# The state-space layer's output projection in three reduced-precision passes, with each group's y turned in the next group

## The reference

```python
zxbcdt = u @ w_in
z, xbc, dt = jnp.split(zxbcdt, [SSD_D_INNER, SSD_D_INNER + SSD_CONV_DIM], axis=-1)
xbc = jax.nn.silu(causal_depthwise_conv(xbc, conv_w, conv_b))
xs, bm, cm = jnp.split(xbc, ...)          # 4 groups: x 512 wide, B and C 128 wide each
...
y = y_diag + y_off + d_skip[:, :, None] * xs
y = y.reshape(bsz, seq, SSD_D_INNER) * jax.nn.silu(z)
y = rms_norm(y.reshape(bsz, seq, g_, SSD_D_INNER // g_), norm_w)   # per group of 512
return y @ w_out                                                   # (512x2048) @ (2048x1024)
...
h = layer_norm(DEEPNORM_ALPHA * x + mix, ln_g[i, 0], ln_b[i, 0])
h = layer_norm(DEEPNORM_ALPHA * h + sq_relu_mlp(h, mlp_w1[i], mlp_w2[i]), ...)
```

## Time and profile before

| | |
|---|---|
| time, median of 3 runs | 2157.13 us (2156.45 to 2160.23) |
| the profiled execution | 2160.06 us, span of its instructions 2158.3 us |
| PE busy with matmuls | 2008.8 us (93%) |
| DVE, ACT, POOL busy | 1040.1, 839.7, 171.7 us |
| mean granted clock of PE | 0.96 |

### The profile page before, as it was taken

The page is one execution under the profiler, slowest core; times in us unless marked ns, Lnnn a source line. Parts: engine busy times, 40 slices in busy tenths (PEclk is TensorE's granted clock), DMA queues, the critical chain, the costliest instruction groups (busy, mean ns, idle before and its releaser), DMA issues.

```text
span 2158.3 us, 26047 instructions
## 1 busy us (share of the span) xinstructions
PE 2008.8 (93%) x9466; PEld 1559.4 (72%) x9466; DVE 1040.1 (48%) x1863; ACT 839.7 (39%) x1703; POOL 171.7 (8%) x137
## 2 busy tenths in 40 slices
PE   8899998999999999988989698999999969989998
PEld 6778786448888887788888677888887745447773
DVE  4665565034444345366677655443436352035643
ACT  5654563023333333365757624232333320114430
POOL 0100110021000003000100021000002000001100
PEclk9999999999999999999999898999999979998999
DMA  4121122222323221241311022232322212110010
GB/s 163 59 98 39 59 98 98 77 72 105 110 85 107 87 104 53 59 118 40 79 39 66 33 78 98 79 117 78 117 78 78 88 51 98 37 65 1 0 39 39
DMA packets 116541, 161.30 MB, mean 75 GB/s; under 512 B 6021, under 2 KB 57059, under 8 KB 116451
## 3 DMA queue, kind: packets, MB, share of 16 engines
q1 hardware_dynamic: 115155, 155.38, 21.6%
q0 software_dynamic: 1296, 4.72, 0.6%
HBM read 157.98 MB, written 2.10 MB: 74 GB/s over the span
## 4 chain that ended last, share of the span: by engine, by line
PE 83%; DVE 8%; ACT 5%; issue 2%; DVEq 1%; DMA 1%; ACTq 0%; SPq 0%; POOLq 0%; POOL 0%
PE psum L900 38%; PE psum L664 9%; PE psum L854 7%; PE psum L985 7%; PE psum L1140 4%; PE psum L629 4%; PE psum L1221 2%; PE psum L1175 2%; PE psum L1017 2%; PE psum L1188 2%; PE psum L964 1%; PE psum L799 1%; ACT fT L1278 1%; DVE w_lo L1938 1%; PE psum L1152 1%
## 5 line engine op out<-in xcount | busy, mean ns | idle before, releaser
L1938 DVE TENSOR_TENSOR w_lo<-slot,w_hi 128x512 fp32r<-128x512 f32 x304 | 213.1, 716 | 382.8 <-ACT w_hi L1421 382.8
L1421 ACT CAST w_hi<-slot 128x512 fp32r<-128x512 f32 x304 | 183.6, 619 | 449.0 <-PE psum L900 448.3
L900 PE MATMUL psum<-f_hi,w_hi 128*128 128x512 f32 (+1 forms) x576 | 215.3, 374 | 19.2 <-DVE f_lo L1945 12.6
L900 PE MATMUL psum<-f_lo,w_hi 128*128 128x512 f32 (+1 forms) x576 | 214.4, 372 | 0.0
L900 PE MATMUL psum<-f_hi,w_lo 128*128 128x512 f32 (+1 forms) x576 | 214.4, 372 | 0.0
L900 PE MATMUL psum<-w_hi,hid_hi 128*128 128x512 f32 x512 | 199.5, 390 | 0.0
L900 PE MATMUL psum<-w_hi,hid_lo 128*128 128x512 f32 x512 | 199.2, 389 | 0.0
L900 PE MATMUL psum<-w_lo,hid_hi 128*128 128x512 f32 x512 | 199.2, 389 | 0.0
L900 PEld LDWEIGHTS psum<-f_hi,w_hi 128*128 128x128 f32 x576 | 112.9, 196 | 38.0 <-DVE f_lo L1945 13.5
L629 PE MATMUL psum<-con,arena 128*128 128x128 f32 (+2 forms) x678 | 105.0, 291 | 33.7 <-ACT arena L1345 13.0
L900 PEld LDWEIGHTS psum<-f_lo,w_hi 128*128 128x128 f32 x576 | 113.0, 196 | 17.3
(11 more groups left out here) (295 smaller groups left out, 4031.7 us busy)
## 6 DMA issues: line engine op xcount, KB each, us to landing
slot<-in_w_mlp SPq DMA_DIRECT2D x128, 512.0 KB, 5.5
slot<-in_w_ssd SPq DMA_DIRECT2D x32, 512.0 KB, 6.3
slot<-in_w_hgrn SPq DMA_DIRECT2D x32, 512.0 KB, 6.6
slot<-in_w_ssd_out SPq DMA_DIRECT2D x16, 512.0 KB, 5.3
slot<-in_w_gate SPq DMA_DIRECT2D x16, 512.0 KB, 5.6
gb<-in_w_ssd SPq DMA_DIRECT2D x8, 512.0 KB, 5.3
slot<-in_w_hgrn_out SPq DMA_DIRECT2D x8, 512.0 KB, 5.2
slot<-in_w_mla SPq DMA_DIRECT2D x8, 512.0 KB, 5.2
```

Source lines behind the costliest of these rows:

```text
L900: m = pe.matmul(psum[:, bank[c], cols or slice(0, HALF)], a, m_, start=k == 0 and n_pass == 0, stop=k == KD - 1 and n_pass == 2)
L1421: act.copy(w_hi[:, k, :], as_k(slot_of(stage, n))[:, k, :]).then_inc(high_made, 1)
L1938: dve.tensor_tensor(w_lo[:, k, :], as_k(slot_of(stage, n))[:, k, :], w_hi[:, k, :].bitcast(F32), ALU.subtract).then_inc(low_made, 1)
```

## The change

Four things change together.

- **The projection** (`ssd_out` in place of `out_and_norm`) is made in three passes. The gain `norm_w` goes into the weights: ACT rounds w times the gain of its row (`out_high`), DVE makes the remainder (`out_low`). Unit 0 takes y of groups 0 and 1 for the first half of the output, by token tile; unit 1 groups 2 and 3, block by block; units 2 and 3 the same for the second half.
- **y** stays in `xr`. Each group's root, reciprocal and normalising are done at the group's end, and PE turns the group's y in the next group behind its first x block (`y_turn`); ACT and DVE copy two chunks each into `yT_a` and `yT_b` (`y_out`). The fourth group's y is turned between units 0 and 1. ACT and DVE split `yT` into high and low parts. `Mh` moves to the memory of `rn`, where y was kept.
- **B and C** are fetched when the group before has begun its first x block, a unit earlier. The sums 0 to 3 stand a block later, and "CB" and "BT" behind the third x block; on DVE the z remainders and the taps of the third x block come ahead of the mask of "CB" and the first four `weights`.
- **Behind the projection** the first MLP unit is split ahead of the last token tile, as at the later layers, and `p` is fetched and turned within the first MLP unit.

The core of the diff:

```diff
@@ banks
+            banks.stage(f"ssd{g}", [("B", 0), ("C", 1), (("x", 0), 2), (("acs", 0), 4), (("acs", 1), 5)]
+                        + [(("yt", c), (6, 7, 0, 1)[c]) for c in range(NT) if g] + [(("x", 1), 3), (("acs", 2), 6), (("acs", 3), 7),
...
+        banks.stage("ssd_out", [((0, t), b) for t, b in enumerate((1, 5, 6, 7))] + [(("yt", c), (4, 2, 3, 4)[c]) for c in range(NT)]
+                    + [((1, t), b) for t, b in enumerate((0, 2, 3, 1))])
-        in_parts = ("mlp0", "gate0", "hgrn_out", "mlp1", "gate1")
+        in_parts = ("ssd_out", "mlp0", "gate0", "hgrn_out", "mlp1", "gate1")
@@ SP
             for g in range(1, S_GROUPS):
+                sp.wait_ge(units_begun, 2 * g - 1)
+                load_bc(g)
                 sp.wait_ge(units_begun, 2 * g)
-                load_bc(g)
                 load_half(g, 0, S_X)
@@ PE
+            def y_turn(stage, g):
+                for c in range(NT):
+                    pe.wait_ge(sig("y_normed"), g * NT + c + 1)
+                    b = claim(stage, ("yt", c))
+                    for k in range(4):
+                        m = turn(b, k * P, xr[:, c, k * P:(k + 1) * P])
+                    m.then_inc(bank_full[b], 1)
...
+                feature_block(("x", 0), "x01", x01, 0, True)
                 spread_sums(0)
                 spread_sums(1)
-                feature_block(("x", 0), "x01", x01, 0, True)
+                if g:
+                    y_turn(stage, g - 1)
+                feature_block(("x", 1), "x01", x01, P, False)
                 spread_sums(2)
                 spread_sums(3)
-                feature_block(("x", 1), "x01", x01, P, False)
+                feature_block(("x", 2), "x23", x23, 0, True)
...
-                feature_block(("x", 2), "x23", x23, 0, True)
                 x_turn(0)
+                feature_block(("x", 3), "x23", x23, P, False)
                 spread_sums(4)
-                feature_block(("x", 3), "x23", x23, P, False)
                 x_turn(1)
...
+            def ssd_out(n, **results):
+                h, part_ = n // 2, n % 2
+                times_parts("ssd_out", n, lambda t, k: (yT_hi[part_][:, k, t * P:(t + 1) * P], yT_lo[part_][:, k, t * P:(t + 1) * P],
+                                                        w_hi[:, k, :], w_lo[:, k, :]),
+                            lambda t: ("ssd_out", (h, t)), opens=part_ == 0, closes=part_ == 1,
+                            ready=None if h else lambda k: pe.wait_ge(sig("yT_low"), part_ * KD + k + 1), **results)
+            for t in range(NT):
+                ssd_out(0, cs=(t,), begins=t == 0, ends=t == NT - 1)
+            y_turn("ssd_out", S_GROUPS - 1)
+            ssd_out(1)
+            ssd_out(2)
+            last_turn = norm_turns("norm00", lambda t: ssd_out(3, cs=(t,), begins=t == 0, ends=t == NT - 1))
@@ ACT
+            def out_high(n, k):
+                if k == 0:
+                    landed(act, "ssd_out", n)
+                if n:
+                    act.wait_ge(blocks_begun, (n - 1) * KD + (k + 2))
+                row = B_SN + (n % 2) * KD + k
+                act.mul(w_hi[:, k, :], as_k(slot_of("ssd_out", n))[:, k, :], col_b[:, row:row + 1]).then_inc(high_made, 1)
@@ DVE, at a group's end
-                    dve.tensor_tensor(ys[c][:, g * HALF:(g + 1) * HALF], ybuf, zs[:, c, :], ALU.mult).then_inc(sig("y_gated"), 1)
+                    dve.tensor_tensor(xr[:, c, :], ybuf, zs[:, c, :], ALU.mult).then_inc(sig("y_gated"), 1)
+                dve.wait_ge(sig("ssq_ready"), NT * (g + 1))
+                dve.tensor_scalar(srs[:, 0, g, :], ssq[:, g, :], 1.0 / HALF, RMS_EPS, ALU.mult, ALU.add).then_inc(sig("sms_ready"), 1)
                 if g + 1 < S_GROUPS:
                     ssd_low(g + 1, "x01")
+                dve.wait_ge(sig("srs_ready"), g + 1)
+                dve.reciprocal(srs[:, 0, g, :], srs[:, 1, g, :])
+                dve.drain()
+                for c in range(NT):
+                    dve.tensor_scalar(xr[:, c, :], xr[:, c, :], srs[:, 0, g, c:c + 1], None, ALU.mult).then_inc(sig("y_normed"), 1)
+                if g + 1 < S_GROUPS:
                     ssd_low(g + 1, "x23")
```

More of the change, by code:

```diff
@@ L474, in slot_free @@
                     sp.sem_inc(sig("slot_given"), 1)
-                elif stage == "mlp0" and n == 1:
-                    wait_full(sp, "ssd_out", NT - 1, NHALF - 1)
                 elif stage == "hgrn_out" or stage == "hgrn" and per:
@@ L537, in _ @@
                     if h == n == 0:
-                        for i in range(DEPTH):
-                            sp.dma_start(s_p[i], p[i].rearrange("(t p) n -> p t n", p=P)).then_inc(p_in, 16)
                         sp.wait_ge(sig("inputs_used"), 1)
@@ L551, in load_mlp @@
                 up(0, 0, 0)
+                if i == 0:
+                    for j in range(DEPTH):
+                        sp.dma_start(s_p[j], p[j].rearrange("(t p) n -> p t n", p=P)).then_inc(p_in, 16)
                 up(0, 1, 0)
@@ L787, in ssd_group @@
                 z_tile(3)
+                if g == S_GROUPS - 1:
+                    wait_taken(pe, stage, ("z", NT - 1))
+                    pe.sem_inc(sig("inputs_used"), 1)
                 wait_taken(pe, stage, "BT")
@@ L863, in times_out @@
                         tile(t)
-            def out_and_norm(stage, norm, left, n_units_):
-                tile = times_out(stage, left, n_units_, 0)
-                for t in range(NT):
-                    tile(t)
-                return norm_turns(norm, times_out(stage, left, n_units_, 1))
-            last_turn = out_and_norm("ssd_out", "norm00", lambda k, t: yT[t][:, k, :], 2)
             inputs_split = [0]
@@ L1493, in ple @@
                         act.activation(sg[:, t, h * HALF:(h + 1) * HALF], psum[:, b, :], ACT.Sigmoid).then_inc(bank_free[b], 1)
-            norm("norm00", B_G, B_B, parts=True, meanwhile=lambda: split_high("mlp0", follows=False))
+            norm("norm00", B_G, B_B, parts=True, before_last=lambda: split_high("mlp0"))
+            for i in range(DEPTH):
+                for k in range(KP):
+                    b = full("p_turn", ("p", i, k))
+                    act.copy(pT[:, i, k, :], psum[:, b, :]).then_inc(bank_free[b], 1)
             mlp(0)
@@ L1822, in ssd_group @@
                 taps(2, ("x", 0), 4 * g)
+                if g:
+                    for c in (1, 3):
+                        y_out(stage, g - 1, c)
                 taps(3, ("x", 1), 4 * g + 1)
+                ssd_low(g, "z")
+                taps(4, ("x", 2), 4 * g + 2)
                 b = full(stage, "CB")
@@ L1854, in ssd_group @@
                     dve.drain()
+                if g == S_GROUPS - 1:
+                    for k in range(KD):
+                        out_low(0, k)
+                        yT_parts(0, k)
                 dve.wait_ge(sig("xD_ready"), g * 4 + 4)
@@ L1980, in mixer_and_norm @@
                     add(t, 0)
+                if between:
+                    between()
                 add_and_norm(add, meanwhile, before_last)
@@ L2041, in ple, with last_out_low @@
                     dve.tensor_tensor(res[:, t, :], res[:, t, :], sg[:, t, :], ALU.add).then_inc(sig(f"ple_done{i}"), 1)
-            mixer_and_norm("ssd_out", lambda: split_low("mlp0"))
+            def last_out_low():
+                for k in range(KD):
+                    out_low(3, k)
+            mixer_and_norm("ssd_out", name=lambda h, t: ((h, t), 0), between=last_out_low,
+                           before_last=lambda: split_low("mlp0"))
             mlp(0)
```

179 lines of the change are left out of this document (90 added, 89 removed), and 10 rows, old and new, of tables (banks, last).

## The result

The changed kernel takes 2133.28 us (median of 4 runs, 2132.06 to 2135.52) against 2157.87 us (median of 4, 2156.45 to 2160.23) for the kernel before: a ratio of 0.9886, 95% interval 0.9869 to 0.9903. It is 24.6 us faster where 35 were forecast; 2133.3 lies 0.3 us above the upper end of the range. The profiled execution took 2132.4 us for a span of 2130.6.

What follows compares the result with a forecast made beforehand. PE matmuls, filling 93% of the span, were taken as the bound. 21.2 + 19.4 - 1.9 - 3.8 = 34.9 us off the profiled 2160.06 gives 2125.2, or 2122 us from the timed median; range 2117 to 2127.

Steps and rivals of the forecast that it cites:

- the term for the groups: Four groups ahead of the projection: their new order, waits and clock together make them 3.8 us longer.
- PE asks for that bank at 157.75, waits 2.6 us, and goes on at 160.35.: Group 1, before z tile 1: PE waits 2.6 us for ACT's evacuation of sum 4, instead of 3.78.
- so I take the full clock behind it in groups 1 and 2.: z tile 1: clock stays full behind the 2.6 us wait, saving 2.3 us in group 1, 1.1 in group 2.
- The new wait at the second x turn: Groups 1 to 3: PE waits 1.6 us for the bank that DVE's mask of B by C must free.
- The product: Output projection: three fp32r passes take 5.57 us a tile; 90.7 us against 111.9, 21.2 us less.
- The tail: From the fourth group's last y product to the projection: 2.4 us replaces 21.8, 19.4 us less; y ready 5.3 early.
- The transition: From the projection's last tile to the first MLP block's second half: 28.61 us against 26.66, 1.9 us more.
- Rival 1: Groups: the clock falls after the shorter waits too, so they cost 7.2 instead of 3.8; 2126 us, chance 0.16.
- Rival 2: Groups: new order costs 4 us more in each of three, one more semaphore wait per DVE step; 2134 us, chance 0.12.
- Rival 3: Groups 1 and 2: wait before z tile 1 goes if DVE takes x3's taps earlier; 2117 us, chance 0.07.
- Rivals 4 and 5: 4: last group's y late for projection, 2125 us, 0.10. 5: y turns wait 15 us in three groups, 2167 us, 0.03.
- The claim that the early fetch gives at most what the new order takes: Groups, before z tile 1: B and C arrive early, but DVE and ACT come 4 us later; group 1 is 1.9 us later.

Runs made afterwards that it cites:

- the first experiment: The changed kernel with x-block 0 times dt moved behind the first four weights on DVE: 2127.0 us, ratio 0.985.
- the one with the mask: Changed kernel with weights behind fourth x block's taps, inputs-used count behind y, and B-by-C mask ahead of z remainders and third x block's taps: 2116.3 us.
- the second experiment: The changed kernel with taps first: DVE's first four weights moved behind the fourth x block's taps and x-block 1 times dt: 2119.1 us, ratio 0.9818.
- the late fetch alone: The changed kernel with the next group's B and C fetched a unit later, as in the kernel before: 2135.55 us, ratio 0.9894.
- the other bank: The kernel of the one with the mask, with y's fourth set of turns in bank 0 and unit 1's first result in bank 4: 2117.1 us.

## Why the prediction was wrong

**The step that failed** is the term for the groups, "3.8 us more". It is 13.1, and the 9.2 between is more than the whole miss in the profiled executions (7.2). In it:

- *"PE asks for that bank at 157.75, waits 2.6 us, and goes on at 160.35."* Counted from the group's B block, PE asked after 47.8 us where 47.7 were forecast, but it went on after 51.6 instead of 50.3. The late part is one row: "one x by dt and four weights (0.7 + 2.5)" is 0.7 + 4.19. I took 2.50 from the earlier trace rows, where POOL stood still beside these weights; in the new order their predecessor starts POOL, and beside it they take 1.69 more. PE's wait is 1.0 to 1.25 us longer than forecast in each group, 4.7 in all, and the first experiment shows the collision as its cause. The Trainium skill, page "SBUF — State Buffer", section "SBUF: two separate sides", says that VectorE with two SBUF inputs and GpSimd take the shared pair of ports in turn, each for a whole instruction. The rows agree: POOL's two instructions end at 151.7 and 153.2, and the two long weights end 0.55 us behind each (152.27 and 153.71), as if each had been held until then for most of its work; beside the taps, with one operand in PSUM, there was no such loss. I had read the order of instructions of the engines one by one and not asked what each of them sets going on another.
- *"so I take the full clock behind it in groups 1 and 2."* It fell behind 3.83, and z tile 1 took 6.76 and 7.75 us instead of 5.55: 1.2 + 2.2 = 3.4 us. Whether it would have fallen behind the forecast 2.6 is open: it fell behind 2.14 in the first experiment and 2.38 in the one with the mask, and held behind 2.29 in group 0 of the changed kernel. "2.6 is nearer to 1.7 than to 3.8" took the clock to go by the length of the wait alone, and between 1.5 and 2.4 us it does not (the last section has the rows).
- *Fourth group.* PE's wait for the last z tile's evacuation, which the change puts ahead of the states, was not in my count: 0.93 us, gone in the experiment that moves it back behind y.
- *The new wait at the second x turn* was 1.03 where I had 1.6: 1.7 us in my favour over three groups. What remains, 1.9 us, lies at 0.6 to 0.9 in each of groups 1 to 3; a part are the turns behind the waits, which at the low clock take 1.03 and 1.11 instead of 0.65, and for the rest I have no run.

**What held.** The product: 5.60 a tile against 5.57; without its two stops the projection took 90.5 us, forecast 90.7. The tail: y of the last group was normalised at 374.4 and asked for at 379.5, 5.1 us to spare where I had 5.3; the 2.4 us in its place were 3.4, since the fourth set of turns waited 1.25 for its bank and not 0.3. The wait for the first result's bank was 0.32 (0.4). The transition took 28.45 (28.6).

**The sum.** 34.9 forecast, less 9.2 for the groups and 0.9 for the projection, plus 0.2 for the transition, 1.7 from a first B block that started earlier (21.15 instead of 22.84) and 1.1 in the rest: 27.8, and 27.7 lie between the spans. The last two terms, 2.8 us, are luck of the two profiled executions: in the profiles of the changed kernel and its seven variants, which are the same up to there, the first B block starts anywhere from 20.10 to 23.29, and the rest differs between them by up to 4.3. The medians differ by 24.6, because the profiled execution of before lay 2.2 above this median and that of after 0.9 below its own. I subtracted a profiled difference from a median and counted on that offset being the same.

**The rivals.** Rival 1, the clock, came true in groups 1 and 2, behind a longer wait than it spoke of. Rival 2 named the effect ("back at 3.8 or more") and a time of 2134, but another cause: not a semaphore more in each step, but four instructions that took 1.7 us longer together, so the near hit of 2134 is luck. The wait at the second x turn, which it had longer, was shorter. Rival 3 did not happen by itself; the second experiment makes it happen by one exchange on DVE, and is worth 14 us. Rivals 4 and 5 did not occur: y was ready everywhere. The claim that the early fetch gives at most what the new order takes held, and the reason for it too: in the changed order no gain can be told (0.4 us in the groups), with the taps first it is worth 19 us, in the kernel before 9.

## What to carry to other kernels

When an instruction is moved, look at whom it releases, not only at whom it waits for: a duration read from a row holds only with the same neighbours running. A transfer brought forward pays only as far as the next thing on the path is ready earlier too, so the two have to be tried together; alone either may read as nothing. And behind a wait of one and a half to two and a half microseconds, carry both outcomes of the clock with weights of the same order: both occurred here behind equal waits, and where the clock was low, z tile 1 took 1.2 to 2.2 us longer.

## What the runs showed of the hardware

**The clock after a short wait is not settled by its length.** Up to the second x turn of group 0 the kernel with the taps first has the same program as the changed kernel. In both PE waits 1.46 us ahead of group 0's first x block, and 2.29 and 2.27 before its second x turn. These are windows behind the two waits, first of the changed kernel, then of the experiment:

```profile
38.00:40.00 2.00, 2.00 (x10) 1.65 (x9) 2.00 (x4) 1.43 (x2) 0.00 (x0) 1.00 0.72 193
68.00:70.00 2.00, 2.00 (x11) 1.61 (x10) 2.00 (x2) 0.00 (x0) 2.00 (x2) 1.00 0.28 37
```

```profile
39.00:41.00 2.00, 2.00 (x6) 1.52 (x6) 2.00 (x4) 1.48 (x2) 0.00 (x0) 0.50 0.50 125
70.00:72.00 2.00, 2.00 (x6) 1.54 (x6) 1.93 (x5) 1.14 (x3) 0.98 (x2) 0.51 0.35 56
```

The same happens at the start of the second half of the first MLP block, where PE waits 1.73 or 1.74 us in the changed kernel (479.65) and in all seven experiments on it. The clock is down behind it in five of them, among them the first (470.02), and up in the changed kernel and in those of the taps first and of the mask. First the changed kernel, then the first experiment:

```profile
481.00:483.00 2.00, 2.00 (x19) 2.00 (x19) 0.69 (x1) 0.67 (x2) 0.00 (x0) 1.00 0.04 8
471.00:473.00 2.00, 2.00 (x12) 2.00 (x11) 0.00 (x0) 0.00 (x0) 0.00 (x0) 0.50 0.00 0
```

From that point to the end the span is 1650.9, 1650.9 and 1651.2 us where the clock stayed up; 1652.2 and 1652.5 where it was soon back (the late fetch alone, the other bank); 1654.9 to 1655.2 in the other three. The work is the same, so one profiled span can carry some 4 us more that have nothing to do with the edit; group lengths were compared here for that reason. What decides the fall at a given wait, no run here shows. Group lengths carry such falls too: the changed kernel was spared both of those in group 0, which the experiment of the taps first had.

**A DVE and a POOL instruction with all operands in SBUF held each other up.** Four weights of 128x512 f32 lost 1.69 us to two POOL instructions of the same size, which themselves took 2.72 instead of 2.09; the whole loss falls on the second and third weight. B and C's four remainders show it as well: 3.82 us with POOL beside them in the changed kernel (157.84), 2.48 with the taps first (154.51), where POOL was done by then.
